# Last expert's rows copied once and added by float32 row tiles; predecessor's rows combined ahead of the last down product; memory means as column tiles

## What is computed

```python
def expert_block(args):                       # first block, 32 experts
    xb, e = args
    gate, up = jnp.split(xb @ w_gate_up[e], 2, axis=-1)
    return (jax.nn.silu(gate) * up) @ w_down[e]
...
y = jnp.zeros((n_tok, D), x.dtype).at[tok_s].add(y_buf[dest] * w_s[:, None])
...
x = layer_norm(DN_ALPHA * x + ffn, ln2_g[l], ln2_b[l])
...
h = jnp.concatenate([meta_b, x], axis=1)      # second block
a = rmsnorm(h, norm_mix[i])
mix = pool_mixer(a, pool_w[j], pool_scale[j])
```

## Time and profile before

| | us |
|---|---|
| median of 3 runs | 1190.19 |
| lowest, highest | 1189.41, 1191.79 |
| the profiled execution | 1190.5 |
| its span | 1189.2 |

### The profile page before, as it was taken

How to read it: one execution, slowest core, us unless ns; L and a number is a source line. 1 busy time by engine, 2 the same in 40 slices (tenths; PEclk the granted TensorE clock), 3 DMA queues, 4 the chain that set the end, 5 groups by cost and what they waited for, 6 DMA issues and landing times.

```text
span 1189.2 us, 21996 instructions
## 1 busy us (share of the span) xinstructions
PE 1054.2 (89%) x9608; PEld 861.8 (72%) x9608; DVE 576.2 (48%) x843; ACT 479.2 (40%) x652; POOL 86.5 (7%) x91
## 2 busy tenths in 40 slices
PE   9999999996676665566678999999999999999998
PEld 8889998663333333333324899999999999999986
DVE  6765777441212121212124676664454548666643
ACT  6655953221111111111124743443357765544433
POOL 0621001000000000000000400000210004000000
PEclk9999999998778889888887999999999999999999
DMA  9843589999999999999999576454534235665520
GB/s 364 320 165 137 188 325 420 401 419 428 427 428 425 427 428 427 427 428 415 429 425 382 174 233 209 156 185 160 190 111 144 90 107 186 222 212 182 183 97 35
DMA packets 104222, 330.31 MB, mean 278 GB/s; under 512 B 4339, under 2 KB 76332, under 8 KB 86334
## 3 DMA queue, kind: packets, MB, share of 16 engines
q1 hardware_dynamic: 102064, 322.77, 70.3%
q10 hardware_dynamic: 1470, 4.02, 0.9%
q0 software_dynamic: 592, 2.10, 0.5%
HBM read 327.82 MB, written 1.06 MB: 277 GB/s over the span
## 4 chain that ended last, share of the span: by engine, by line
PE 66%; DMA 29%; DVE 2%; ACT 2%; issue 1%; SPq 0%; DVEq 0%; ACTq 0%
DMA wide<-in_w_gate_up_dram 18%; PE PS L489 13%; PE PS L490 13%; PE PS L491 13%; DMA wide<-in_w_down_dram 11%; PE PS L1229 5%; PE PS L858 4%; PE PS L504 2%; PE PS L852 2%; PE PS L505 2%; PE PS L506 2%; PE PS L1385 1%; PE PS L838 1%; DMA raw<-in_w_in_dram 1%; PE PS L1162 1%
## 5 line engine op out<-in xcount | busy, mean ns | idle before, releaser
L1992 DVE TENSOR_TENSOR lo<-raw,hi 128x2048 fp32r<-128x2048 f32 (+1 forms) x111 | 253.2, 2285 | 147.3 <-ACT hi L1477 118.8
L1477 ACT CAST hi<-raw 128x2048 fp32r<-128x2048 f32 (+1 forms) x109 | 204.0, 1875 | 111.1 <-PE PS L491 74.3
L489 PE MATMUL PS<-AH,hi 128*128 128x256 f32 (+1 forms) x816 | 232.3, 285 | 1.0 <-DVE AL L2496 1.0
L490 PE MATMUL PS<-AL,hi 128*128 128x256 f32 (+1 forms) x816 | 229.9, 282 | 0.0
L491 PE MATMUL PS<-AH,lo 128*128 128x256 f32 (+1 forms) x816 | 229.8, 282 | 0.0
L858 PE MATMUL PS<-wide,XS 128*32 128x256 f32 x1568 | 129.2, 486 | 81.9 <-DMA wide<-in_w_gate_up_dram 79.8
L858 PEld LDWEIGHTS PS<-wide,XS 128*32 128x32 f32 x1568 | 56.3, 133 | 142.6 <-DMA wide<-in_w_gate_up_dram 98.3
L489 PEld LDWEIGHTS PS<-AH,hi 128*128 128x128 f32 x816 | 153.7, 188 | 2.3 <-issue 1.0
L490 PEld LDWEIGHTS PS<-AL,hi 128*128 128x128 f32 x816 | 153.7, 188 | 0.4
L491 PEld LDWEIGHTS PS<-AH,lo 128*128 128x128 f32 x816 | 153.7, 188 | 0.0
L2424 DVE TENSOR_TENSOR Y<-PS,Y 32x256 fp32r<-32x256 f32 x128 | 53.9, 421 | 123.1 <-ACT Y L1689 120.1
(11 more groups left out here) (447 smaller groups left out, 1845.1 us busy)
## 6 DMA issues: line engine op xcount, KB each, us to landing
wide<-in_w_gate_up_dram SPq DMA_DIRECT2D x49, 2048.0 KB, 45.5
wide<-in_w_down_dram SPq DMA_DIRECT2D x25, 2048.0 KB, 45.5
raw<-in_ffn_w_gate_dram SPq DMA_DIRECT2D x22, 1024.0 KB, 5.6
raw<-in_ffn_w_up_dram SPq DMA_DIRECT2D x22, 1024.0 KB, 5.7
raw<-in_w_in_dram SPq DMA_DIRECT2D x21, 1024.0 KB, 8.4
raw<-in_ffn_w_down_dram SPq DMA_DIRECT2D x19, 1024.0 KB, 4.9
spare<-in_w_gate_up_dram SPq DMA_DIRECT2D x14, 1024.0 KB, 14.4
raw<-in_sb_w_qkv_dram SPq DMA_DIRECT2D x12, 1024.0 KB, 5.1
```

Of the source, the lines that this page charges most:

```text
L489: pe.matmul(o, w(h, c), xh(k), start=start and c == c0, stop=False)
L490: pe.matmul(o, w(h, c), xl(k), start=False, stop=False)
L1477: act.copy(K.view(K.hi[i % HN], 0, [[1, n]]), K.view(K.rbuf[i], 0, [[1, n]])).then_inc(S.hi, 1)
L1992: r = e.tensor_tensor(K.view(K.lo[i % HN], 0, [[1, n]]), K.view(K.rbuf[i], 0, [[1, n]]), K.view(K.hi[i % HN], 0, [[1, n]]).bitcast(F32), A ...
```

## The change

- `first_means()` is called ahead of unit j = 0 of `up(31)` instead of j = 2, and each of its eight matmuls becomes four with 32 stationary columns, on the four column tiles.
- The rows of expert 30 are combined alone: `one_combine()`, four matmuls as in `combine`, stands in `down(31)` between its two units. `slot` column 15 is -1 for the rows of expert 31. VectorE's `pick(15)` moves ahead of `store(30)`.
- The rows of expert 31 are copied once by ScalarE, as they stand in the bank, in float32 (`YL`, 128x256). VectorE no longer stores them. `last_combine()` adds them with eight float32 matmuls of 256 columns, each with 32 stationary rows, on the four row tiles; the second four wait until the first four have ended. Their one-hot matrix `SELL` repeats the slot in each row block; VectorE's `pick_last()` writes it at the end of expert 30.
- The statistics wait for the new counts of `S.comb`, and two waits of `pe_second` for the count of `y_lo` that is still reached.

```diff
-               ("masks", 8 * 128), ("iota", 256), ("slot", 16), ("iota4", 4), ("iota32", 32)):
+               ("masks", 8 * 128), ("iota", 256), ("slot", 17), ("iota4", 4), ("iota32", 32)):
...
-    put("slot", 2 * KEEP * np.arange(16)[None, :] + KEEP * (p[:, None] >= 64) + p[:, None] % KEEP)
+    slot = 2 * KEEP * np.arange(17)[None, :] + KEEP * (p[:, None] >= 64) + p[:, None] % KEEP
+    slot[64:, 15] = -1
+    slot[:, 16] = KEEP * (NE - 1) + p % KEEP
+    put("slot", slot)
...
+    K.YL = K.SW
+    K.SELL = K.SS[0]
...
-            if e == NE - 1 and j == 2:
+            if e == NE - 1 and j == 0:
                 first_means()
...
             if i == K.P0 - 1:
+
+                one_combine()
...
+    def one_combine():
+
+        pe.wait_ge(S.y_lo, 4 * (NE - 1))
+        pe.wait_ge(S.pick, 17)
+        for i in range(2):
+            for c in range(2):
+                pe.matmul(bank(2 * i + c, 0, [1, 512]), view(K.SEL, 128 * i, [[1, 128]]), view(K.Y, 512 * c, [[1, 512]]),
+                          start=False, stop=False, skip_group_check=True)
+
     def last_combine():
 
-        pe.wait_ge(S.pick, 16)
-        for c in range(2):
-            pe.wait_ge(S.y_lo, 4 * NE - 2 + 2 * c)
-            for i in range(2):
-                pe.matmul(bank(2 * i + c, 0, [1, 512]), view(K.SEL, 128 * i, [[1, 128]]), view(K.Y, 512 * c, [[1, 512]]),
-                          start=False, stop=True, skip_group_check=True).then_inc(S.comb, 1)
+        pe.wait_ge(S.y_hi, 4 * (NE - 1) + 1)
+        for n in range(2):
+            if n:
+                pe.wait_ge(S.comb, 34)
+            for i, c in ((0, n), (0, 2 + n), (1, 1 - n), (1, 3 - n)):
+                pe.matmul(bank(2 * i + c // 2, 256 * (c % 2), [1, 256]), view(K.SELL, 128 * i, [[1, 128]], 32 * c, 32),
+                              view(K.YL, 0, [[1, 256]], 32 * c, 32), start=False, stop=True, skip_group_check=True).then_inc(S.comb, 1)
...
         for k in range(8):
-            r = pe.matmul(bank(PB, 2 * NMETA * k, [1, 2 * NMETA]), view(K.MT, 128 * k, [[1, 128]], rows=NMETA),
-                          view(K.PMM, 2 * NMETA * (k // 2), [[1, 2 * NMETA]], rows=NMETA), start=True, stop=True)
+            for c in range(4):
+                r = pe.matmul(bank(PB, 2 * NMETA * k, [1, 2 * NMETA], p0=32 * c, rows=32), view(K.MT, 128 * k + 32 * c, [[1, 32]], rows=NMETA),
+                              view(K.PMM, 2 * NMETA * (k // 2), [[1, 2 * NMETA]], rows=NMETA), start=True, stop=True)
...
         act.wait_ge(S.unit, K.at["dn", (e, 1)] + 1)
+        if e == NE - 1:
+            act.copy(view(K.YL, 0, [[1, 256]]), bank(down_bank(e), 0, [1, 256])).then_inc(S.y_hi, 1)
+            return
...
+    def pick_last():
+
+        to = lambda c: view(K.DSTB, 128 * c, [[256, 2], [1, 128]])
+        two = lambda x: view(x, 0, [[128, 2], [1, 128]])
+        slot = K.con("slot", 16, 1)
+        dve.wait_ge(S.gat, gathered(8))
+        a = own(dve.tensor_scalar(two(K.SS[1]), to(0), slot, None, ALU.is_equal))
+        own.wait(dve, a)
+        dve.scalar_tensor_tensor(two(K.SELL), to(1), slot, two(K.SS[1]), ALU.is_equal, ALU.add).then_inc(S.pick, 1)
+
...
             if e == NE - 1:
                 turn(e)
+                pick(15)
             store(e - 1)
...
+        if e == NE - 2:
+            pick_last()
...
-    if e1 == NE:
-        pick(15)
-        store(NE - 1)
...
         for c in range(2):
-            dve.wait_ge(S.comb, 31 + i + 2 * c)
+            dve.wait_ge(S.comb, 35 + 2 * i + c)
             r = dve.bn_stats(st(i, 6 * c, 6), bank(2 * i + c, 0, [1, 512]))
```

More of the change, by code:

```diff
@@ L1031, in turn @@
         else:
-            pe.wait_ge(S.y_lo, 4 * NE)
+            pe.wait_ge(S.y_lo, 4 * (NE - 1))
             pe.wait_ge(S.ht, NE)
```

## The result

The changed kernel took 1195.3 us (median of 7, 1192.55 to 1197.58) beside 1190.19 for the kernel before, measured with it (median of 7, 1189.39 to 1193.03). The ratio on record is 1.0031, 95% interval 1.0021 to 1.0042: slower by 0.31%. It is not the quotient of the two medians, which would be 1.0043. Two later comparisons gave 1.0032 (1.0017 to 1.0047) and 1.0009 (1.0000 to 1.0019). Over all executions of all comparisons the medians are 1192.7 (33) and 1189.8 us (107), a difference of 2.9 us, or 0.25%.

What follows compares the result with a forecast made beforehand. Experts wait for weights up to 630 us, then TensorE and the takers of its results bound the kernel. A 2.05 us gain and 2.09 us cost put statistics at 649.40 against 649.36: 0.0 us, 1190.2 us, range 1188.8 to 1192.3.

Steps and rivals of the forecast that it cites:

- D: End of the down product of expert 30: 644.30 us before, forecast 642.25, bounds 641.8 and 643.6.
- The first part brings 2.05 us.: Up to the end of expert 30's down product: shorter, earlier means and an earlier clock rise gain 2.05 us.
- rival 3: A little faster: weight transfers set the end of expert 30's down product, at 641.8; -0.45 to -0.9 us; chance 0.15.
- the means at 631.6: Ahead of expert 31's products: 64 matmuls wait for scaled memory rows until about 631.6, then take 1.4 us.
- the clock's rise inside the products of 31: Clock rises at 637.3, 4.3 us after expert 31's products start; they end at 638.8 instead of 640.7.
- rival 2: A late clock rise or badly overlapping row tiles: +1.4 us each, about 1191.6; chance 0.15.
- The second costs 2.09 us.: From the end of expert 30's down product to the statistics: 7.15 us instead of 5.06, a cost of 2.09.
- wait for expert 30's low parts: Between the last down product's halves, combining waits for expert 30's subtractions until 2.37 us after its down product ends.
- combining to product: In the last down product: four 512-column combining matmuls take 1.19 us, the next matmul starting some 0.2 before their end.
- fills: Ahead of the last combining: six matmuls, 1.56 us, of which 0.75 us is not covered by ScalarE's copy.
- The time at which the statistics start is passed on to the end nearly whole.: Behind the statistics: TensorE runs block after block from 654.2, so a shift in their start reaches the end nearly whole.
- rival 1: Slower: the means keep 3.6 us at the low clock; +2.2 to +3.6 us, 1193.1; chance 0.10.

Runs made afterwards that it cites:

- b1: The kernel before, unchanged, profiled a second time; the profiled execution took 1189.38 us.
- b2: The kernel before, unchanged, profiled a third time; the profiled execution took 1189.53 us.
- a4: The kernel before with only the new means at unit 0, last rows as before: 1189.84 us, ratio 1.0004.
- a1: The changed kernel as it is, profiled and timed again: 1192.72 us (median of 10), ratio 1.0032.
- a3: The changed kernel with the old eight wide means restored at unit 2, so only the last rows change: 1193.29 us, ratio 1.0029.
- c1: The changed kernel with the three fills ahead of last_combine() moved behind it and three more behind first_units(): 1190.25 us, ratio 1.0010.
- c2: c1 with the combining of expert 30 moved behind the last down product: 1189.98 us, ratio 1.0006.
- d1: c1 without its six fills behind the last down product: 1191.65 us (median of 11), ratio 1.0010.
- a2: The changed kernel with two fills added behind last_combine() and three behind first_units(): 1193.57 us (median of 12), ratio 1.0021.

## Why the prediction was wrong

It gave 1190.2 with a range to 1192.3, and "no change" at 0.84. The measured time is 1195.3, and 1192.7 over all executions. The time of the statistics, on which the sum was made, was right to 0.1 us, and that was luck: D came 0.8 us earlier than its 642.25, the part behind it took 0.86 us longer than its 7.15, and the two errors cancel. What failed:

- **"The first part brings 2.05 us."** D did move to 641.46 (landing 639.55 plus 1.9). But the old D of 644.30 belonged to one execution with a low clock for 20 us; in b1 D is at the landing plus 1.9 already, in b2 at plus 3.3. In all seven executions of the changed kernel D was at the landing plus 1.9, which is the bound of rival 3 (the transfers set D); the rest of its path, the means at 631.6 and the clock's rise inside the products of 31, was not what happened. What I called a sample of one for the clock's rise (rival 2) I had not applied to the base of the comparison. Even against the execution of rows 1 to 8 the old rows could have used only 1.5 of the 2.05, as a4 shows, since their last product then waits for its last quarter.
- **"The second costs 2.09 us."** From D to the statistics it took 8.01, not 7.15. The wait for expert 30's low parts was right (2.36 against 2.37). Too small by 0.10 to 0.15 each: combining to product 1.13 (1.0), half product 1.00 (0.85), fills 1.49 (1.35), first to second row-tile group 0.88 (0.78). From the second group's start to the statistics it was 1.15 and not 0.77. Row tiles in themselves cost what the L632 row said: 0.71 for eight.
- **"The time at which the statistics start is passed on to the end nearly whole."** This step failed in kind. I looked at which instruction waits for which, and not at what a hole in TensorE's work does to its clock. The old combining was still running at 650.1, 2.6 us ahead of the turn at 652.77; the new one ends at 649.0, 3.9 us ahead of its turn. With that the clock fell in seven executions of seven, at a price of 0.5 to 2.1 us; with the old combining it fell in one of three, for 0.1. No rival had it; rival 1 was a slow clock in another place.
- **The means** took 0.75 us in the changed kernel, and not 1.4, because the clock was high there. In a1 the clock was low, and they took 1.08:

```profile
629.94 1.08 PE L950 MATMUL PS<-PMM,MT 16*32 16x32 f32 x64 [2.44 <-ACT MT L1742]
```
```profile
629.90:631.10 1.20, 1.16 (x68) 1.10 (x72) 1.13 (x4) 1.20 (x1) 0.00 (x0) 0.50 0.96 410
```

So rival 1 (3.6 us at the low clock) is out by its own condition. The rule of the Trainium skill, "TensorEngine Tiling (Array Packing)", section "Instruction Overhead", would make it some 1.6 us for the 64 even at the 2.4 GHz level, an estimate; the trace, with 0.75 us, disagrees.

Added up against the landing of expert 30's weights, from there to AH: 25.2 us on average over the three profiled executions of the kernel before, 27.8 over the seven of the changed kernel. That is 2.6 us, where the medians of all executions differ by 2.9.

That the rows' new order costs time is shown by a3 against a4, and where the later statistics come from by the profiles of c1 and c2. That the idle time lets the clock fall is shown by the profiles of the kernels with fills and of d1, not by their times. a3, without a fall, and b2, with one, say that neither the new rows nor the old ones decide it in each execution; what else does is open. Open too is the rest of the 5.1 us of the first comparison. Its longest executions (up to 1197.58) were never caught with a profile. The wide spacing of matmuls, worth 2.6 to 4 us, was seen in a2 and d1; whether it makes these executions, and what selects it, the runs don't tell.

## What to carry to other kernels

Before an earlier or later step is credited in microseconds, take a second profile of the kernel before and measure both from the landing that feeds the stage: a gain over one execution's low clock is no gain. Where work is taken from TensorE just ahead of its next long block, look at the hole that is left: matmuls that nobody reads cost nothing in it, and here they brought back 0.5 to 2.1 us of the stage. Fills that covered a wait must be moved when the wait is removed; left in place they were the largest part (0.93 of 1.95 us) of the later statistics. An agreement of a sum with a time is no support for its terms: here two errors of 0.8 and 0.86 us cancelled.

## What the runs showed of the hardware

- The granted clock fell at 652.3 (first profile; 652.0 to 656.5 in the seven), in a stretch of 3.70 us in which TensorE was busy for 1.07; with 3.86 of 4.00 it stayed. It isn't fixed by that: a3, busy for 1.07 of 3.80 us, kept its clock. What a fall costs hangs on what it meets: 2.07 us where it lay over the sixteen products (5.53 us in place of 3.62), 0.10 where it ended as they began (b2).
- A stream of equal matmuls at granted clock 1.00 has more than one pace. In the second feed-forward part one matmul of 256 columns started every 113 ns in all but one of the profiled executions, and every 118 in the other, for over 100 us (532 against 512 in 60 us); in the first part 109 against 106 of a line stood in 40 us.
- Sixty-four matmuls with 16 rows, 32 stationary and 32 moving columns took 0.75 us with their loads at the high clock, 12 ns each, and 1.08 at the low one (a1).
